# Attention kernel: keys before the mean, the rotary sum two steps later, the third Newton operation one step earlier in VectorE's written order

## The reference

```
q = rms_norm(q_lat) @ w_q_b ; kv = rms_norm(kv_lat) @ w_kv_b      # 16 heads
k = concat(k_nope, k_pe broadcast to all heads)                    # 64 + 32
q = rms_norm(q, q_gain) ; k = rms_norm(k, k_gain)                  # per head, over 96
q, k = rotary on the last 32 of each
s = q @ k.T * 96**-0.5, causal over keys 0..e, e = 144, 272, 400, 528
o = softmax(s) @ v ; out = concat(o over heads) @ w_out
```

## Time and profile before

| | |
|---|---|
| median of 3 runs | 2742.28 us (2736.22 to 2743.20) |
| the profiled execution | 2742.57 us, span 2740.8 us |
| busy, share of the span | PE 96%, PEld 82%, DVE 45%, ACT 36%, POOL 34% |
| TensorE's granted clock, mean | 0.98 of full speed |
| steps 0 to 7 of the 8 pairs | about 2088 to 2341 us of the span |

### The profile page before, as it was taken

How to read it: one execution, slowest core, us unless ns; L and a number is a source line. 1 busy time by engine, 2 the same in 40 slices (tenths; PEclk the granted TensorE clock), 3 DMA queues, 4 the chain that set the end, 5 groups by cost and what they waited for, 6 DMA issues and landing times.

```text
span 2740.8 us, 36067 instructions
## 1 busy us (share of the span) xinstructions
PE 2635.8 (96%) x15144; PEld 2248.0 (82%) x15144; DVE 1229.7 (45%) x1689; ACT 980.4 (36%) x1495; POOL 931.5 (34%) x381
## 2 busy tenths in 40 slices
PE   7999999899999997999999999999988999999999
PEld 5777778677777786899999899999976777788887
DVE  6444442354444407678877431111245675422111
ACT  4333333333333323344444432322324454333222
POOL 3343344243343341222332234434421000244443
PEclk9999999999999998999999999999998999999999
DMA  4233232233333231112221223333321000133332
GB/s 135 87 111 94 89 110 85 69 104 94 90 109 93 88 100 47 54 56 63 62 62 55 62 77 100 86 93 86 93 66 32 16 24 17 55 114 93 92 94 91
DMA packets 61329, 215.66 MB, mean 79 GB/s; under 512 B 8176, under 2 KB 8560, under 8 KB 61168
## 3 DMA queue, kind: packets, MB, share of 16 engines
q1 hardware_dynamic: 57248, 202.05, 25.0%
q10 hardware_dynamic: 3920, 11.31, 1.3%
HBM read 211.24 MB, written 2.10 MB: 78 GB/s over the span
## 4 chain that ended last, share of the span: by engine, by line
PE 90%; DVE 7%; ACT 1%; issue 1%; DMA 0%; POOL 0%; DVEq 0%; ACTq 0%
PE psum L364 75%; PE psum L458 1%; PE psum L468 1%; PE psum L651 1%; PE psum L974 1%; PE psum L654 1%; PE psum L940 1%; PE psum L913 1%; PE psum L606 1%; PE psum L938 1%; PE psum L376 1%; PE psum L976 1%; PE psum L917 1%; PE psum L665 1%; DVE sb_scale L1537 1%
## 5 line engine op out<-in xcount | busy, mean ns | idle before, releaser
L344 POOL TENSOR_TENSOR sb_w_lo<-sb_w_raw,sb_w_hi 128x1024 fp32r<-128x1024 f32 x377 | 931.3, 2473 | 1787.2 <-ACT sb_w_hi L1094 1787.1
L364 PE MATMUL psum<-sb_h_hi,sb_w_hi 128*128 128x512 f32 (+1 forms) x2648 | 822.3, 352 | 48.6 <-DVE sb_h_lo L1546 32.3
L364 PE MATMUL psum<-sb_h_lo,sb_w_hi 128*128 128x512 f32 (+1 forms) x2648 | 794.4, 341 | 0.0
L364 PE MATMUL psum<-sb_h_hi,sb_w_lo 128*128 128x512 f32 (+1 forms) x2648 | 790.9, 340 | 0.0
L1094 ACT ACTIVATE sb_w_hi<-sb_w_raw 128x1024 fp32r<-128x1024 f32 x377 | 395.5, 1054 | 604.3 <-PE psum L364 457.2
L364 PEld LDWEIGHTS psum<-sb_h_hi,sb_w_hi 128*128 128x128 f32 x2648 | 459.0, 190 | 124.2 <-issue 35.6
L364 PEld LDWEIGHTS psum<-sb_h_lo,sb_w_hi 128*128 128x128 f32 x2648 | 457.7, 190 | 62.4 <-issue 7.0
L364 PEld LDWEIGHTS psum<-sb_h_hi,sb_w_lo 128*128 128x128 f32 x2648 | 457.9, 190 | 56.2
L364 PE MATMUL psum<-sb_mix_hi,sb_w_hi 128*128 128x264 f32 (+1 forms) x1424 | 420.8, 341 | 10.2 <-POOL sb_w_lo L344 5.6
L364 PE MATMUL psum<-sb_mix_lo,sb_w_hi 128*128 128x264 f32 (+1 forms) x1424 | 413.7, 336 | 0.0
L364 PE MATMUL psum<-sb_mix_hi,sb_w_lo 128*128 128x264 f32 (+1 forms) x1424 | 412.5, 335 | 0.0
(11 more groups left out here) (275 smaller groups left out, 2585.8 us busy)
## 6 DMA issues: line engine op xcount, KB each, us to landing
sb_w_raw<-in_weights SPq DMA_DIRECT2D x377, 512.0 KB, 3.6
sb_decay<-in_decay ACTq DMA_DIRECT2D x16, 640.0 KB, 3.9
sb_resid<-in_x SPq DMA_DIRECT2D x4, 512.0 KB, 9.0
out<-sb_resid SPq DMA_DIRECT2D x8, 256.0 KB, 2.1
sb_table<-in_rope_table ACTq DMA_DIRECT2D x1, 264.0 KB, 3.4
sb_s<-in_positions ACTq DMA_DIRECT2D x1, 256.0 KB, 7.3
sb_cols<-in_cols ACTq DMA_DIRECT2D x1, 158.5 KB, 4.6
sb_ones<-in_ones ACTq DMA_DIRECT2D x1, 64.0 KB, 5.7
```

The lines of the kernel that those rows point to most:

```text
L344: e.tensor_tensor(g.w_lo[:, u % 4, :], g.w_raw[:, u % 2, :], g.w_hi[:, u % 4, :].bitcast(F32), ALU.subtract).then_inc(S["w_lo"], 1)
L364: mm = e.matmul(g.psum[0:m, at + b, 0:wd], w[:, slot, P * i:P * i + m], xs[:, tile, c:c + wd], start=first and n == 0, stop=last and n == 2)
```

## The change

Only the written order in `dve_mla` changes. Four edits:

- step 2 loses the rotary sum of the next pair and gains Newton part 2 of this pair's head 1;
- step 3 loses Newton part 2 and holds only the keys of head 1;
- step 4 gains the rotary sum;
- step 6 gains keys part 0 of the next pair's head 0; in step 7 keys part 1 stands ahead of the mean of head 1 and no longer behind it.

```
-            if n == 2:
+            if n == 4:
                 dve_pair_turn(g, e, pair + 1, 2)
...
                     dve_pair_newton(g, e, pair + 1, 0, part)
+                dve_pair_keys(g, e, pair + 1, 0, 0)
             if n == 7:
+                dve_pair_keys(g, e, pair + 1, 0, 1)
                 dve_pair_mean(g, e, pair + 1, 1)
-                dve_pair_keys(g, e, pair + 1, 0, 0)
-                dve_pair_keys(g, e, pair + 1, 0, 1)
         if n == 2:
-            dve_pair_newton(g, e, pair, 1, 0)
-            dve_pair_newton(g, e, pair, 1, 1)
+            for part in range(3):
+                dve_pair_newton(g, e, pair, 1, part)
         if n == 3:
-            dve_pair_newton(g, e, pair, 1, 2)
             dve_pair_keys(g, e, pair, 1, 0)
             dve_pair_keys(g, e, pair, 1, 1)
```

## The result

| | before | changed kernel |
|---|---|---|
| median of 10 runs each | 2742.93 us | 2729.08 us |
| lowest to highest | 2736.22 to 2756.10 | 2725.75 to 2730.44 |
| profiled execution, its span | 2742.57, 2740.8 us | 2728.05, 2726.2 us |
| granted clock, mean over the span | 0.982 | 0.984 |

The ratio is 0.9942, with a 95% interval of 0.9930 to 0.9955: 0.6% faster. It is estimated from all runs; the medians alone give 0.9950, since the kernel before has a few runs far above its median. The forecast, 2735.3 us, called within 0.3% the likeliest; the measured time is that of its rival A, 2729.5 us. The runs also lie closer together than before, 4.7 us against 19.9.

The account below looks back on a forecast made before the run. TensorE's own work was taken to bound 90% of the span, its waits for keys being 10.4 us. Terms of 3.24 + 0.2 + 0.66 + 2.75 + 0.45 = 7.3 us off 2742.57 gave 2735.3 us, range 2728.5 to 2740.5.

Parts of the forecast that it names:

- rival A: TensorE's clock comes out better: one long and one short slow stretch in the pairs go, 2729.5 us; chance 0.20.
- Step 4: In pairs 2 to 7, scores for the keys of head 1 start 0.54 us earlier, 3.24 us together.
- Pair change: Scores of the next pair's step 0 start 0.55 us earlier, then held by ScalarE's copy; five times, 2.75 us.
- First and last pair: First pair: 0.2 us at step 4 and 0.55 us at its pair change; last pair: 0.66 us at step 4.
- What was costed at nothing: Output operation of step 4 and mean of head 1 come later, covered by 1.6 and 0.4 us: no cost.
- The sum of the waits: Over all pairs, 3.24 + 0.2 + 0.66 + 2.75 + 0.45 = 7.3 us off 2742.57 us.
- The clock: TensorE's slow stretches in the pairs: no term in the sum; changes left to rival A and rival C.
- rival C: Clock comes out worse: shorter pairs shift their thin places, adding slow stretches; 2750.1 us at four long ones; chance 0.05.
- Rival B: The pair change's gain is given back before step 2's scores, only step 4's terms stay: 2738.5 us; chance 0.13.
- The rule of the Trainium skill against the edit: Last pair, step 3: GpSimd, starting later, could delay VectorE's scaled maximum, making the 0.66 us term near 0.
- The rule of the Trainium skill on small idle times: Small idle times between TensorE's matmul groups can make its clock go back and forth; would favour rival A; no size.

Follow-up runs that it names:

- e2: Only the change's edits of steps 6 and 7, made to the kernel before; 2746.46 us, ratio 0.9997 to before.
- e7: Changed kernel, scores of steps 0 and 4 waiting for ScalarE's small copy, not the large one behind it; 2728.10 us, ratio 0.9935 to before.
- e3: Kernel before, with two spare TensorE products ahead of its waits for the keys in steps 0 and 4; 2733.57 us, ratio 0.9954 to before.
- e5: Kernel before, with two spare TensorE products ahead of its wait for the keys in step 4 alone; 2734.42 us, ratio 0.9943 to before.
- e6: Kernel before, with two spare TensorE products ahead of its wait for the keys in step 0 alone; 2745.30 us, ratio 0.9982 to before.
- e8: Changed kernel, with ScalarE's rounding of the next weights moved from step 1 to step 4; 2728.02 us, ratio 0.9918 to before.
- e1: Only the change's edits of steps 2, 3 and 4, made to the kernel before; 2731.01 us, ratio 0.9951 to before.
- e4: Changed kernel, with five spare TensorE products ahead of the scores of step 4; 2736.74 us, ratio 0.9965 to before.
- e9: Changed kernel with the edits of e7 and e8 together; 2726.37 us, ratio 0.9931 to before.

## Why the prediction was right or wrong

- **Step 4, 0.54 us in each of six pairs: right.** Pairs with this edit alone went from 30.06 to 29.50 us.
- **Pair change, 0.55 us, bound by ScalarE's copy: right.** Handing over took 0.12 us and not 0.05; e2's pairs gained 0.48. e7 showed that the copy was the binding condition.
- **First and last pair, 0.2 + 0.55 and 0.66: near.** 0.74 and 0.55.
- **What was costed at nothing: right.** No block waits for the output operation in step 5 or for the mean in step 0.
- **The sum of the waits, 7.3 us: 6.9 measured.** The mechanism was right. TensorE's idle time in a pair shrank less than rival A says ("by more than half"): from 1.8 to 1.0 us.
- **The clock, 0 us in the sum: wrong, and this is the step that failed.** The forecast kept the slow stretches as they were and gave their going a chance of 0.20. It was 7.0 us, as large as all the waits. e3, e5 and e6 showed that the wait before step 4 is what costs clock: filling it, with no start earlier, took 10 us off the median of before, and filling the one at step 0 nothing. How it does so is shown for place A alone, 2.8 of the 7.0 us. The other 4.2 us are the stretch at place B, and why the changed kernel's traces lack it stays open, since other kernels without the wait still fell there. Rival A had this mechanism, and its 2729.5 us lies 0.4 us from the median, in part by luck: it counted two slow pairs (3.7 and 1.6 us, with 0.55 of a covered pair change), and three were slow; the window of 32.25 us was not among its rows. What spoke against it, "the same waits stood in pairs that ran at 1.00", was weak: a wait that makes the clock fall only at times leaves most pairs at 1.00. The loads would have told more than the means by pair: two of three stretches began within 0.5 us of the start of scores that had waited before step 4.
- **"Nothing in the change makes TensorE idler" (rival C): true, but not the whole of it.** In e2 less idle time at step 0 went with more time at the lower clock. Idle time at one place, before step 4, was what counted, not its sum.
- **Rival B** didn't happen in the changed kernel. Its mechanism, a gain at step 0 given back at an exponential, showed in e7, for a third of the gain.
- **The rule of the Trainium skill against the edit** (an operation of VectorE with two SBUF inputs and one of GpSimd exclude each other, SBUF — State Buffer, "SBUF: two separate sides") agrees with e8. The scaled maximum stretches to GpSimd's end wherever the two meet: in step 2 of the changed kernel it takes 0.95 us, and in e8 that of step 5 takes 0.52 us, for which nobody waits before the last pair. The rule didn't spoil the last pair's term: GpSimd's operation and the 1.35 us of the scaled maximum stayed as they were.
- **The rule of the Trainium skill on small idle times** (TensorE: Matmul & The Clock Gate, "A second HAM failure mode: psum-queue depth-cycling") had the right direction. The same page's table "Why this matters for your kernels" warns only of far longer idle gaps. Here falls came behind one of 0.46 us, and at place B behind no wait for another engine, so the measurement decides.

Open: why the same program of before ran in two groups (in one set of 30 runs, 16 at 2739 to 2744 us and 14 at 2748 to 2758), though two traces of the upper group had 41 and 48 us of slow stretches in the pairs and one of the lower 17. Open too: why e1, e4, e5, e7, e8 and e9 met place B while the changed kernel, in two traces, did not. The runs show where the clock fell and what stopped it at place A, not when it falls at such a place and when not.

## What to carry to other kernels

Where TensorE bounds a kernel and its clock dips, list the beginnings of the slow stretches and look at what TensorE did just before them; a short wait beside thin products (few columns each) can cost more in clock than in waiting. To tell the two apart, fill the wait with spare products that nobody reads: if the time falls though nothing starts earlier, it is the clock. When a wait is taken away, name the next condition of the same instruction; here a copy that had been hidden took half of the second gain.

## What the runs showed of the hardware

In the pairs the granted clock fell from 1.0 to 0.5 in stretches of 3.4 to 17 us while TensorE was busy for over 90% of the time. At place A it had, in 12 of 14 falls, made sums with one column and then waited about 0.5 us (0.46 in the kernel before). The kernel before had 17, 48 and 41 us at 1.2 GHz in the pairs in its three traces, at 2742.57, 2756.61 and 2754.64 us. Two spare products of 128 columns in that wait (e3, e5) left no fall at A in either trace. At place B the clock fell with no wait for another engine, behind the same kind of sums and products of 16 and 64 columns. With one or two spare products of 128 columns (0.2 us each) ahead of it, two traces had no fall there; that these ended it is not shown.
